# Latent attention with turned products: divided probabilities, values stationary in 64 columns

## The reference, cut to what matters

```
def block(i):
    sc = (jnp.einsum('bqhd,bkhd->bhqk', q_block(q_nope, i), k_nope)
          + jnp.einsum('bqhr,bkr->bhqk', q_block(q_rope, i), k_rope)) * scale
    sc = jnp.where(chunk_causal_mask(i, seq), sc, NEG_INF)
    p = jax.nn.softmax(sc, axis=-1).astype(v.dtype)
    return jnp.einsum('bhqk,bkhd->bqhd', p, v)
...
o = jnp.concatenate([o_mla.reshape(b, seq, -1), o_diff.reshape(b, seq, -1),
                     o_fox.reshape(b, seq, -1)], axis=-1)
return o @ w_out
```

## Time and profile before

| what | value |
|---|---|
| runs (3) | median 2170.95 us, 2169.5 to 2171.2 |
| profiled execution, from first to last instruction (span) | 2168.2 us |
| what lies around the span, against the median of the runs | 2.75 us |
| PE busy | 2073.7 us (96%) |
| DVE busy | 1492.0 us (69%) |
| ACT busy | 1216.6 us (56%) |
| latent units of the first layer | about 126 to 162 us of the span |
| latent units of the second layer | about 601 to 635 us of the span |

### The profile page before, as it was taken

One profiled execution on the slowest core, in us unless ns is written; L12 is line 12 of the kernel. 1 busy time (PEld: TensorE's weight loads), 2 busy tenths in 40 slices (PEclk: granted clock), 3 DMA queues, 4 the chain that ended last, 5 costly groups with the idle time before them and its releaser, 6 DMA issues.

```text
span 2168.2 us, 28287 instructions
## 1 busy us (share of the span) xinstructions
PE 2073.7 (96%) x10192; PEld 1728.0 (80%) x10192; DVE 1492.0 (69%) x2053; ACT 1216.6 (56%) x1926; POOL 49.4 (2%) x64
## 2 busy tenths in 40 slices
PE   7988999998998999999999999999999999899999
PEld 5777888877776888878888988788888887778887
DVE  6568999996658999987554758555555457665554
ACT  4544777874635777765444665654444445465443
POOL 0000000000000000001000000000000001000000
PEclk9998999998998999999999999999999999899999
DMA  6223999993235999976555453455555655234553
GB/s 249 85 79 135 366 362 349 373 356 102 97 100 195 367 370 358 360 272 201 191 191 193 140 175 115 139 169 189 186 175 194 191 189 192 72 117 155 191 187 109
DMA packets 124199, 446.55 MB, mean 206 GB/s; under 512 B 14320, under 2 KB 15472, under 8 KB 123120
## 3 DMA queue, kind: packets, MB, share of 16 engines
q1 hardware_dynamic: 124048, 444.61, 59.4%
HBM read 443.51 MB, written 1.05 MB: 205 GB/s over the span
## 4 chain that ended last, share of the span: by engine, by line
PE 50%; ACT 2%; DVE 2%; issue 0%; POOL 0%; DVEq 0%; ACTq 0%
PE bank L1212 7%; PE bank L1211 7%; PE bank L1220 7%; PE bank L1244 4%; PE bank L1242 4%; PE bank L1243 4%; PE bank L640 3%; PE bank L643 3%; PE bank L641 3%; PE bank L1190 1%; PE bank L2877 1%; PE bank L2838 1%; PE bank L2879 1%; PE bank L2878 1%; PE bank L2859 1%; PE bank L687 1%
## 5 line engine op out<-in xcount | busy, mean ns | idle before, releaser
L596 DVE TENSOR_TENSOR lo<-stage,hi 128x1024 fp32r<-128x1024 f32 (+1 forms) x834 | 970.3, 1206 | 248.4 <-ACT hi L584 199.4
L584 ACT ACTIVATE hi<-stage 128x1024 fp32r<-128x1024 f32 (+1 forms) x834 | 831.7, 1043 | 235.7 <-PE bank L1244 112.8
L1211 PE MATMUL bank<-hi,thi 128*128 128x512 f32 x704 | 278.5, 396 | 0.0
L1212 PE MATMUL bank<-lo,thi 128*128 128x512 f32 x704 | 274.9, 391 | 0.0
L640 PE MATMUL bank<-hi,thi 128*128 128x512 f32 (+3 forms) x584 | 231.6, 397 | 9.0 <-ACT thi L1675 3.3
L641 PE MATMUL bank<-lo,thi 128*128 128x512 f32 (+3 forms) x584 | 224.8, 385 | 0.0
L2506 PE MATMUL bank<-hi,scr_r 128*128 128x512 f32 x512 | 206.8, 404 | 9.0 <-issue 6.8
L643 PE MATMUL bank<-hi,tlo 128*128 128x512 f32 (+3 forms) x584 | 208.0, 383 | 0.0
L1220 PE MATMUL bank<-hi,tlo 128*128 128x512 f32 x704 | 203.0, 390 | 0.0
L2508 PE MATMUL bank<-hi,scr_r 128*128 128x512 f32 x512 | 202.1, 395 | 0.0
L2507 PE MATMUL bank<-lo,scr_r 128*128 128x512 f32 x512 | 201.6, 394 | 0.0
(11 more groups left out here) (405 smaller groups left out, 2836.7 us busy)
## 6 DMA issues: line engine op xcount, KB each, us to landing
stage<-in_exp SPq DMA_DIRECT2D x384, 512.0 KB, 5.2
stage<-in_ffn SPq DMA_DIRECT2D x264, 512.0 KB, 4.2
stage<-in_wi_a SPq DMA_DIRECT2D x16, 512.0 KB, 6.1
stage<-in_wi_b SPq DMA_DIRECT2D x16, 512.0 KB, 4.4
stage<-in_mem_wkv SPq DMA_DIRECT2D x16, 512.0 KB, 5.3
stage<-in_xwq SPq DMA_DIRECT2D x16, 512.0 KB, 4.4
stage<-in_xwo SPq DMA_DIRECT2D x16, 512.0 KB, 4.5
stage<-in_ssd_xbc SPq DMA_DIRECT2D x12, 512.0 KB, 3.8
```

What stands on the lines that cost most here:

```text
L584: a.activation(self.hi[i % NR][:, x:y], self.stage[(2 * i + p) % (2 * NS)][:, :y - x], ACT.Copy).then_inc(*c.tick(("hi", i, p), sem="hi"))
L596: v.tensor_tensor(self.lo[i % NR][:, x:y], self.stage[(2 * i + p) % (2 * NS)][:, :y - x], self.hi[i % NR][:, x:y].bitcast(F32), ALU.subtra ...
L1211: t.matmul(out, self.thi[:, xs], hi[:, ws], start=(k == 0), stop=False)
L1212: t.matmul(out, self.thi[:, xs], lo[:, ws], start=False, stop=False)
```

## The change

Only units 5 to 7 of each mixer take the new path (`"turned" in unit`).

- (u,3) on DVE: for each half of the heads, a reciprocal of its sums and a multiplication of its 512 columns of exponentials in `sc` (`prob`). PE's four transposes of a half wait for that half. ACT still copies bank 4, DVE bank 5.
- (u,4) on PE: the values are stationary (64 columns) and `pt` moves (128 columns). An even head writes rows 0 to 63 of the bank, an odd head rows 64 to 127, so that the product comes out with features on the rows.
- (u,4) on ACT: the bank is copied, rounded, into `thi`; on DVE: the remainder goes into `tlo` and marks (S,"o",u).
- After the attention: `turn_pe`, `turn_act` and `turn_dve` for "oa" are gone.

```diff
             elif p == 3:
                 for n in range(H * nt // 4):
                     prior = [(S, "pt", w, n) for w in range(u) if units[w]["nb"] > n][-1:]
-                    for w in c.need((S, "exp", u), prior or free[2]):
+                    for w in c.need((S, "prob", u, n) if "turned" in unit else (S, "exp", u), prior or free[2]):
                         t.wait_ge(*w)
...
+            elif p == 4 and "turned" in unit:
+                bank = self.bank[PAIRS[u % 2][0]]
+                for i in range(H // 2):
+                    for w in c.need([(S, "pt", u, n) for n in range((i * nt + nt + 1) // 2)]):
+                        t.wait_ge(*w)
+                    for k in range(nt):
+                        for j in (2 * i, 2 * i + 1):
+                            m = t.matmul(bank[j % 2 * 64:j % 2 * 64 + 64, i * 128:(i + 1) * 128], unit["v"](j, k),
+                                         pt[u % 2][:, (j * nt + k) * 128:(j * nt + k + 1) * 128],
+                                         start=(k == 0), stop=(k == nt - 1))
+                m.then_inc(*c.tick((S, "pv", u)))
...
+            elif p == 3 and "turned" in unit:
+                hn = H // 2
+                for n in range(2):
+                    sn = s[:, n * hn:(n + 1) * hn]
+                    for w in c.need((S, "exp", u, n)):
+                        v.wait_ge(*w)
+                    v.reciprocal(sn, sn).then_inc(*c.tick())
+                    for w in c.need(c.last):
+                        v.wait_ge(*w)
+                    x = r3(sc[u % 2][:, n * 512:(n + 1) * 512], nk)
+                    v.tensor_tensor(x, x, bc(sn, 2, nk), ALU.mult).then_inc(*c.tick((S, "prob", u, n)))
+                for w in c.need((S, "pT", u, 1), (S, "o", u - 2)):
+                    v.wait_ge(*w)
+                v.tensor_copy(pt[u % 2][:, 512:1024], self.bank[5][:, :]).then_inc(*c.tick((S, "pt", u, 1)))
+            elif p == 4 and "turned" in unit:
+                hi, lo, k0, tt0, done = unit["turned"]
+                hi, lo = (r3(x, T)[:, k0:k0 + H // 2, tt0:tt0 + 128] for x in (hi, lo))
+                for w in c.need((S, "ohi", u)):
+                    v.wait_ge(*w)
+                v.tensor_tensor(lo, r3(self.bank[PAIRS[u % 2][0]][:, :H * 64], 128), hi.bitcast(F32), ALU.subtract).then_inc(
+                    *c.tick((S, "o", u), done))
...
+            elif p == 4 and "turned" in unit:
+                hi, lo, k0, tt0, done = unit["turned"]
+                for w in c.need((S, "pv", u)):
+                    a.wait_ge(*w)
+                a.activation(r3(hi, T)[:, k0:k0 + H // 2, tt0:tt0 + 128], r3(self.bank[PAIRS[u % 2][0]][:, :H * 64], 128),
+                             ACT.Copy).then_inc(*c.tick((S, "ohi", u), self.rounded(done)))
...
-        self.turn_pe(t, c, S, "oa", lambda tt: R["o_mla"][tt], 4, (S, "o", 7), ev(wo_b, 1), b0=6)
...
-        self.turn_act(a, c, S, "oa", 4, b0=6)
...
-        self.turn_dve(v, c, S, "oa", 4, b0=6)
```

More of the change, by code:

```diff
@@ L983, in attention_pe, with attention_dve @@
             yield
-    def attention_dve(self, v, c, S, units, pt, st2=None, lean=False, order=None):
+    def attention_dve(self, v, c, S, units, pt, st2=None, lean=False, order=None, sc=None):
         for u, p in order or self.parts(len(units)):
@@ L1067, in attention_act @@
                     a.activation(sc[u % 2][:, j * nk:(j + 1) * nk], ps, ACT.Exp, bias=b[:, j:j + 1], scale=scale,
-                                 accum_out=s[:, j:j + 1]).then_inc(*c.tick((S, "exp", u)))
+                                 accum_out=s[:, j:j + 1]).then_inc(*c.tick((S, "exp", u), (S, "exp", u, 2 * j // H)))
                 if "sink" in unit:
@@ L1449, in mixer_rooms @@
         R["lb"] = [proj[tt][:, 0:512] for tt in range(2)]
-        R["o_mla"] = self.room(q_at, 512, 2)
         R["o_diff"] = [self.gb_[:, 1152 + 256 * tt:1408 + 256 * tt] for tt in range(2)]
@@ L1505, in unit @@
             return dict(tt=tt, heads=heads, nk=nk, nb=len(heads) * (tt + 1) // 4, dv=64,
-                        **kind, mask=self.maskr[:, m + 256 - nk:m + 256], out=out[tt][:, h0 * 64:(h0 + ng) * 64], **kw)
+                        **kind, mask=self.maskr[:, m + 256 - nk:m + 256], out=out and out[tt][:, h0 * 64:(h0 + ng) * 64], **kw)
         def vals(src, h0, two=1):
@@ L1521, in mixer_units @@
         for tt, hs in ((0, range(8)), (1, range(4)), (1, range(4, 8))):
-            units.append(unit(tt, list(hs), R["o_mla"], 128, kT, qT, lambda h: (0, 96, h * T), scale=96 ** -0.5,
+            units.append(unit(tt, list(hs), None, 128, kT, qT, lambda h: (0, 96, h * T), scale=96 ** -0.5,
+                              turned=(self.thi[:, :4 * T], self.tlo[:, :4 * T], hs[0] // 2, tt * 128, (S, "oa", "lo", hs[0] // 4)),
                               ready=[self.heads(S, "hq", 8), *[(S, "hk", "ev", n) for n in range(6)]],
@@ L1991, in side @@
                 yield
-        mixed(self.attention_dve(v, c, S, self.mixer_units(l, S), R["att"][2:4], self.gb_, lean=True, order=self.ORDER),
-              side(), self.BESIDE)
+        mixed(self.attention_dve(v, c, S, self.mixer_units(l, S), R["att"][2:4], self.gb_, lean=True, order=self.ORDER,
+                                 sc=R["att"][0:2]), side(), self.BESIDE)
         c.end((S, "att"))
-        self.turn_dve(v, c, S, "oa", 4, b0=6)
         self.router_gains_dve(v, c, l)
```

## The result

| kernel | median us (runs) | lowest to highest | span of the profiled execution |
|---|---|---|---|
| before, beside it | 2169.18 (7) | 2166.2 to 2171.2 | 2168.2 |
| changed | 2175.33 (7) | 2174.42 to 2184.54 | 2173.5 |

The changed kernel is slower: 1.0036 times the time before [1.0024, 1.0049], some 6 to 8 us. The forecast was 2174.2, slower by 3.2. It was added to 2170.95, the median of three runs of the kernel before. So 2175.33 lies 1.1 us from its number, while the change itself came out two to two and a half times as large as forecast.

The account below looks back on a forecast made before the run. PE was taken to bound the kernel, so mixer delays move the end equally. Terms summed to +3.15 us in the second layer and +0.05 in the first, together +3.2 on 2170.95: 2174.2 us, range 2169.0 to 2180.5.

Parts of the forecast that it names:

- rival 3: Second layer's clock gets no new low stretch: 2172.9 us, down to 2169.4 if the first layer's ends sooner; chance 0.20.
- unit 5's detour: Division delays unit 5's transposes, ACT's copy and unit 7's scores: +1.5 us in the second layer, +0.2 in the first.
- clock behind it: Second layer: after PE's 2.6 us wait for unit 7's scores, the clock falls for 3.6 us of work: +1.8 us.
- unit 6's transposes: They wait for DVE's divisions: +0.85 us at full clock, charged +0.3 at half clock.
- product, unit 6: Unit 6's product on two column halves, partly side by side, takes 1.3 us: -0.57 us a layer.
- unit 7's transposes: They wait for DVE's multiplications, queued behind its residual addition: +2.1 us for each layer, the largest term.
- product, unit 7: Unit 7's product on two column halves, partly side by side, takes 1.3 us: -0.57 us a layer.
- transposes gone: End of attention: without eight transposes `wo_a` follows `wo_b` directly, -1.4 us for each layer.
- The term for the product: Products on column halves in units 6 and 7: 16 passes at 0.081 us, 1.3 us, so -0.57 us each.
- Rival 4: One half's load can't run beside the other half's product: 0.16 us a pass, product 2.6 us, 2181.2 in all; chance 0.05.
- rival 1: Column halves don't overlap, products stay near 1.7 us: 2.4 us more, 2176.6 in all; chance 0.22.
- Rival 2: Clock also falls after PE's stall at unit 7's transposes: 1.8 us for each layer, 2177.8 in all; chance 0.18.

Follow-up runs that it names:

- e4: Changed kernel with all heads of units 6 and 7 written to rows 0 to 63, one after another; 2177.82 us, ratio 1.0051 to the kernel before.
- e7: The changed kernel run again without an edit; 2178.78 us, ratio 1.0043 to the kernel before.
- e3: Changed kernel with ACT copying unit 5's product before unit 6's exponentials instead of behind them; 2173.66 us, ratio 1.0031 to the kernel before.
- e5: Changed kernel with unit 5's product copied before unit 6's exponentials and units 6 and 7 divided early; 2162.86 us, ratio 0.9976 to the kernel before.
- e6: As e5, with the last six products of `wo_b`'s first turn before unit 6's product; 2161.70 us, ratio 0.9977 to the kernel before.
- e8: e6 with all heads of units 6 and 7 on rows 0 to 63; 2168.07 us, ratio 0.9999 to the kernel before.
- e9: e6 without reciprocals and multiplications in units 5 to 7; 2160.62 us, ratio 0.9969 to the kernel before.
- e1: Changed kernel without reciprocals and multiplications of the exponentials in units 5 to 7; 2168.86 us, ratio 1.0012 to the kernel before.
- e2: Changed kernel with unit 7's two divisions right behind its exponentials on DVE, ahead of the residual additions; 2172.40 us, ratio 1.0023 to the kernel before.

## Why the prediction was right, and where it was off

It was right in its direction and in the waits it named, and short in its size. The 1.1 us between 2174.2 and 2175.33 are partly luck: the forecast stood on a median of three runs of the kernel before, 2170.95, and with four more runs it was 2169.18. Against that the change cost 6.2 us by the medians and 7.8 by the ratio, where +3.2 was forecast. Of the 5.3 us between the two profiles some 3.5 lie in the latent units, which is what the forecast summed. The range, 2169.0 to 2180.5, held (its lower end is rival 3's 2169.4, with 0.4 more that nothing accounts for).

The second layer, step by step, as PE's delay against before, from the mask product at 602.4 (1.0 us late on entry) on:

| step | forecast | measured | how it is read |
|---|---|---|---|
| unit 5's detour | +1.5 | +1.36 | scores at 616.92 for 614.56, less 1.0 |
| clock behind it | +1.8 | +1.67 | first product of `wo_b` at 620.69 for 616.66 |
| unit 6's transposes | +0.3 | +0.21 | 1.00 us to the next product, was 0.79 |
| product, unit 6 | -0.57 | -0.59 | from the last product of `wo_b` before it to the first after it 1.35, was 1.94 |
| unit 7's transposes | +2.1 | +1.96 | from PE's own time for them, 628.70, to the next product 2.95, was 0.99 |
| product, unit 7 | -0.57 | -0.59 | 1.34, was 1.93 |
| transposes gone | -1.4 | -1.38 | 0.22 from last to first, was 1.60 |
| sum | +3.15 | +2.64 | |

Every term is within 0.15 us, though nearly all err to the same side, 0.5 together, and the clock fell where it was said to. The forecast read 3.6 us at 1.2 GHz from rows 3; both profiles have 3.4 in the second layer's stretches, which makes the 1.67.

**The term for the product was right by two errors.** Its text gave 0.081 us for a pass; over the whole product it is 0.064, and 0.055 inside it, close to the lower bound, 0.85 us for 16. The row it came from has the same rate: in the trace rows 9's eight passes also start in pairs, 0.007 us apart, the later pairs 0.11 us from each other. Its edges were shared out over eight passes instead of 16, and that made 0.081. The text also compared 1.3 us from first pass to next product with 1.89 to the last end, where 1.70 is the like. The true gain from first to next is 0.67, and 0.09 of it goes for a pause ahead of the first pass: 0.32 us behind the product before, usually 0.23. The Trainium skill (TensorEngine Tiling (Array Packing), Theoretical Speedup) gives up to twice the rate for a dimension of 64. The passes agree, 0.109 us in e4 for 0.055; the product with its edges has 1.8. Rival 4, which rested on a load of the other half being laid bare, has no support in any run, nor has rival 1.

**The first layer failed: +0.05 forecast, +0.90 measured.** Two terms of it did. "+0.2" for unit 5's detour was +0.73: I let the product decide, with the exponentials of unit 6 ending at 138.22 as before. They stand on ACT behind the copies of side work, which stand behind the transposes, so the 0.5 us counted in the second layer holds here too, and more at half clock; relative to PE's entry (0.8 us early) they ended 1.1 us later, at 138.52. "And rises after the wait, as before: nothing" was wrong about the clock. It rose before the product (1.09 us where the forecast said 2.6), and after PE's wait of 2.69 us it fell again, and that low stretch lasted longer than before. From the first product of `wo_b` to unit 6's transposes PE took 4.01 us (143.86 to 147.87), before 3.26 (143.93 to 147.19): +0.75. Unit 6's "+0.3" was nothing there. The rest agrees: 2 times -0.59, +1.96, -1.39.

**The rest of the 5.3 us of the spans** lies outside the latent units. PE was 0.8 us early at 126 us, before anything that the change touches; that was gone by 168 us, then +1.0 at 601 (where it came from is not shown), +3.6 at 644, +4.8 at 690, and 5.1 to 5.7 from 1000 us on. The step of 1.2 us between 644 and 690 is a low stretch of the clock at the start of the experts. With a window's clock between 1 and 0.5 as the share of it at either level, the windows from 676 to 682 us before (0.77, 0.50, 0.88) make 3.4 us at 1.2 GHz, those from 678 to 686 now (0.65, 0.50, 0.50, 0.65) 6.8 us. That the mixer's shift caused this is not shown.

**Rivals 2 and 3.** Rival 2 said that the clock also falls behind unit 7's stall. In the first profile it did not. In e7's profile of the same code it did, in both layers, with 3.4 us at 1.2 GHz or 1.7 us each, close to the 1.8 that the rival asked for; so some executions of this kernel pay it and some don't, and it is part of their spread. Rival 3, a clock that is kept, fell for the changed kernel, but e3, e5, e6, e8 and e9 show it at the scores: with a wait of 1.4 us instead of 2.4 to 2.7 the clock did not fall behind them.

The view "slower" as a whole is borne out by what the runs take away: without the division 5 to 6.5 us less, with division and copy moved 13 less. The edit's own gains, products (2.4 us) and transposes (2.8), were there all the time and paid for by DVE's place in the order and the clock.

Open is why e9's and e6's spans and medians differ by different amounts (2.8 and 1.1 us). The runs' clocks spread by more than that.

## What to carry to other kernels

When a scaling moves from behind a product to ahead of its transposes, its instructions enter the path of the bound engine: place them right behind what makes their input, ahead of anything on that queue that nobody waits for. Look at both ends of a moved copy as well, since a unit's copy standing behind the next unit's exponentials cost more than the saved product gave; and mend such waits together, because one alone can do no more than move PE up to the next (e3). A price for one pass taken from a short run of passes has the run's edges in it: eight passes gave 0.081 us, sixteen give 0.064, and the pitch inside is 0.055 in both. A change that adds DVE work may still win if all of it stands early: e6 takes 0.9977 of the time before, the change as given 1.0036.

## What the runs showed of the hardware

- Float32 passes with 64 stationary columns, in turn on the two column halves and on the same 128 rows, start in pairs 0.007 us apart, a pair every 0.109 us; in one half (e4, e8) a single pass every 0.109, in the whole array before every 0.112. With the edges a product of 16 takes 1.03, 1.89 and 1.70 us to the next product. The Trainium skill (TensorE: Matmul & The Clock Gate, The mechanism) lets a load overlap only a matmul in another row group; these runs don't agree with that, since both halves are on the same rows and the loads of a pair (at 626.24) begin while the passes before it (626.18 to 626.51) are under way.
- Going over from whole-array products to halves costs PE about 0.09 us: 0.32 us from the last product to the first pass, usually 0.23. The way back shows too: 0.20 us from the last pass to the next product, 0.08 before, with PEld idle for 0.17 us in front of its load.
- Behind PE's waits of 2.2 to 2.8 us at the scores (changed kernel, e1, e2, e4, e7) the granted clock fell in nine cases of nine, behind e1's 1.82 and behind the ten of 1.42 to 1.43 (e3, e5, e6, e8, e9) in none. Behind the 1.50 at unit 6 (e3) it fell in one layer of two, where the product took 1.74 us, and behind the 1.58 at unit 7 (changed kernel, e3, e4, e7) in three cases of eight. The wait's length alone doesn't settle it.
- The same code spread from 2174 to 2186 us, with its mean granted clock from 0.982 to 0.973. A gain of 5 us in this kernel needs ten or so runs.
